# Attention probabilities turned by VectorE and DMA instead of by TensorE

## The chip, the cores and the metric

One Trainium2 chip, one core of it. The metric is the device time of one execution in microseconds (us). The core's engines run in parallel, each through its own queue in order: TensorE (PE in the rows, with its weight loads as PEld), VectorE (DVE), ScalarE (ACT), GpSimd (POOL) and SyncE (SP), which issues most DMAs. They wait for one another through semaphores.

## The reference

One block on x of 512 positions by 2048 channels, in fp32, depth 1:

```
h = rms_norm(x);  q, k, v, g_a, u_p, g_p = split(h @ w_in)           # six widths of 1024
q, k = rms_norm per 64 channels, then a partial rotation by position
s_c = q_c k_c^T / 8;  p_c = softmax(s_c)          # 8 heads, two halves c = 0, 1 of 64 channels
a = p_0 - lam * p_1;  o = a @ v;  attn = rms_norm(o) * 0.8
pool = (centred_mean(u_p, window) - u_p) @ w_pool * pool_scale        # windows 2, 4, 8, 16
out = x + concat(attn * silu(g_a), pool * silu(g_p)) @ w_out
```

## The kernel before

**Precision.** Every fp32 operand of a product is split in two: ScalarE writes a rounded high part (fp32r), VectorE the rest as a low part, and TensorE does three products (high x high, low x high, high x low) instead of one. So each tile of weights costs ScalarE one cast of 128 x 512 and VectorE one subtraction.

**Halves.** Weights come in blocks of 512 KB (`raw`, four slots) and are split in halves of 128 x 512 into four slots (`w_hi`, `w_lo`). One half feeds twelve products of 128 x 512 on TensorE. ScalarE's split of half m + 3 waits until TensorE has ended half m - 1 (semaphore `w_used`), since it takes that half's slot.

**Stages.** First V for all heads (32 halves), then K of the first round (8), then four rounds over m = 8 ... 47. A round has five groups of 8 halves: Q, U (the pool's input), GA, GP (the gates), and K of the next round, each into two PSUM banks. In the last round the output product begins in place of K; then follow six more passes of it.

**A round's attention.** Two heads of four query tiles make eight items. They are woven between the halves by hand: each engine has a loop over m with tests on m. Before the change, item i goes like this:
- TensorE, after half 24 + 2i: the scores of the 128 queries against 512 keys, 4 products into banks S0 and S0 + 1 (`scored`). They wait for the exponentials of item i - 1 (`exp_done`), which read the same banks.
- VectorE, m = 25 + 2i: the row maximum (L1063) and its scaling (L1064).
- ScalarE, m = 26 + 2i: behind the split of half m + 3 (L685) the cast at_hi of item i - 1 (L799), and then two exponentials with row sums (L806, item i).
- VectorE, m = 27 + 2i: reciprocal, coefficient, scaling by a vector (L1044), and p_0 - lam p_1 (L1046).
- TensorE, after half 27 + 2i: four transposes of 128 x 128 into bank TB (L584).
- VectorE, m = 28 + 2i: at_lo (L1070).

After half 35 and after half 43 TensorE multiplies the four turned items of a head with V (12 products). After half 39 it does the pool's 12 products, and at m = 40 it waits for VectorE's evacuation of GP's bank (L926) before K's first half. The sums for K and Q are normalised and rotated by VectorE up to m = 22 (L958 to L965), and SyncE copies parts of Q and K to the other 64 partitions (L347 to L357).

**Start.** TensorE runs 16 products on ones (L452). SyncE issues x in parts of 512 KB and 1 MB (L286), V's weights (L293), and then twelve DMAs of constants (L329, L331) before it goes on with V's weights. The row of epsilons is spread by one fp32 product (L625) and copied by VectorE.

All products but these go through one helper (L457).

Of the kernel before, what the change touches and what calls it, by code (L numbers as in the profile page):

```python
# [6 lines left out]
F32 = mybir.dt.float32  # L7
# [16 lines left out]
def hybrid_block(nc, x, x_cols, norm_w, w_in, q_norm_w, k_norm_w, lq1, lk1, lq2, lk2, subln_w, w_pool,  # L24
                 pool_scale, w_out, identity, pair_ones, rope_cos, rope_sin, inv_count, out):
# [34 lines left out]
    with ExitStack() as ctx:  # L60
# [28 lines left out]
        q_stack, q_stack_at = fixed("q_stack", [P, 2, 2, SEQ], F32R)  # L89
        kh_twice, _ = fixed("kh_twice", [P, 2, 2, SEQ], F32R)  # L90
        kl_twice, _ = fixed("kl_twice", [P, 2, 2, SEQ], F32R)
        diff, diff_at = fixed("diff", [P, 2, 2, SEQ], F32R)
        at_hi, at_hi_at = fixed("at_hi", [P, ST, SEQ], F32R)
        at_lo, _ = fixed("at_lo", [P, ST, SEQ], F32R)
        work, work_at = fixed("work", [P, 5 * 2 * XW])
        wp_raw, wp_raw_at = fixed("wp_raw", [P, 512])
        inv_cnt, inv_cnt_at = fixed("inv_cnt", [P, SEQ])
# [3 lines left out]
        wp_hi, _ = fixed("wp_hi", [P, 512], F32R, at=inv_cnt_at)  # L101
# [3 lines left out]
        wide_b, _ = fixed("wide_b", [P, KP - RAW_SLOTS, HN], at=at_hi_at)  # L105
# [8 lines left out]
        hsq_hi, hsq_lo = kh_twice[:, 0, 1], kl_twice[:, 0, 1]  # L114
# [7 lines left out]
        x_eps = sb("x_eps", [P, ST])  # L122
        nw = sb("nw", [P, KT])
        cos_t = sb("cos_t", [P, SEQ])
        sin_t = sb("sin_t", [P, SEQ])
        ident = sb("ident", [P, P])
# [16 lines left out]
        row_max = sb("row_max", [P, 2])  # L143
# [3 lines left out]
        coef = sb("coef", [P, 1])  # L147

# [42 lines left out]
        eps_diag, ones_f32 = probs[:, 0, :], gate[:, 0, 0:P]  # L191
        rstd_line = head_out[0:1, :]
# [14 lines left out]
        x_in = [sem(f"x_in{i}") for i in range(5)]  # L207
        x_row_in = [sem(f"x_row_in{i}") for i in range(ST)]
        rstd_squared = sem("rstd_squared")
        eps_diag_ready, eps_spread, eps_row_ready = sem("eps_diag_ready"), sem("eps_spread"), sem("eps_row_ready")  # L210
        x_rstd_ready, rstd_line_in, rstd_spread = sem("x_rstd_ready"), sem("rstd_line_in"), sem("rstd_spread")
        sums_raised, gate_ready, pool_gate_ready = sem("sums_raised"), sem("gate_ready"), sem("pool_gate_ready")
        ident_in, k_moved = sem("ident_in"), sem("k_moved")
# [7 lines left out]
        wp_in, inv_in, scale_in = sem("wp_in"), sem("inv_in"), sem("scale_in")  # L221
# [6 lines left out]
        scored, max_ready, exp_done, attn_ready = sem("scored"), sem("max_ready"), sem("exp_done"), sem("attn_ready")  # L228
        at_transposed, at_hi_ready, at_lo_ready = sem("at_transposed"), sem("at_hi_ready"), sem("at_lo_ready")
# [32 lines left out]
        def form_count(p, pair):  # L262
            return (KP // 2) * p + pair + 1

# [19 lines left out]
        def _(sp):  # L284
# [30 lines left out]

            load_x_cols(0, 0, 2)
            load_v(0)
            load_x_cols(1, 2, 4)
            load_v(1)
            load_x_cols(2, 4, 8)  # L320
            load_v(2)
# [993 lines left out]
```

## Time and profile before

| | us |
|---|---|
| median of 3 runs | 777.97 (777.52 to 778.23) |
| the profiled execution, its own time | 778.13 |
| its span in the profile | 776.3 |
| TensorE busy | 769.8 |
| VectorE busy | 551.0 |
| ScalarE busy | 381.6 |
| GpSimd busy | 31.3 |

The span runs from the first to the last instruction; the profiled execution takes 1.8 us more than its span. Busy times overlap. The granted clock is full in every slice of the page. A product of 128 x 512 shows as some 390 ns, but products overlap and follow one another every 0.23 us.

### The profile page before, as it was taken

The numbers are of one execution on the slowest core, as the hardware profiler recorded it, in microseconds if no ns is written. First come the engines' busy times: TensorE is split into PE (matmuls) and PEld (weight loads), VectorE is DVE, ScalarE is ACT, GpSimd is POOL, SyncE is SP. The second block draws the span as 40 slices with busy tenths as digits, with TensorE's granted clock in tenths as the row PEclk, the third lists the DMA queues.
The fourth block names the chain that finished last, engine by engine and source line by source line (L and its number), as shares of the span: only waits on it lengthen the run. The fifth ranks groups of instructions, "written<-read, shape, count | busy, mean of one in ns | idle before, by whom it ended". The sixth has DMA issues, their size and how long they took to land.

```text
span 776.3 us, 9638 instructions
## 1 busy us (share of the span) xinstructions
PE 769.8 (99%) x3458; PEld 637.0 (82%) x3458; DVE 551.0 (71%) x861; ACT 381.6 (49%) x649; POOL 31.3 (4%) x42
## 2 busy tenths in 40 slices
PE   9999999999999999999999999999999999999997
PEld 8788888888888888888888888888888888888886
DVE  5543235888854788985478897348888869987796
ACT  5463134444474354455354355554345665655552
POOL 0010000000000000000000000000000003322200
PEclk9999999999999999999999999999999999999999
DMA  9853323452222354221234421224432169999972
GB/s 333 327 194 92 98 89 102 135 156 70 74 73 64 109 149 126 78 81 55 81 110 147 122 81 57 79 78 139 140 105 81 56 233 255 276 275 263 211 168 108
DMA packets 67079, 106.22 MB, mean 137 GB/s; under 512 B 5344, under 2 KB 46560, under 8 KB 66528
## 3 DMA queue, kind: packets, MB, share of 16 engines
q1 hardware_dynamic: 60288, 86.72, 34.6%
q0 software_dynamic: 4736, 16.78, 11.0%
q10 hardware_dynamic: 2016, 2.18, 0.9%
q8 instruction: 27, 0.44, 0.2%
q14 instruction: 12, 0.10, 0.0%
HBM read 95.17 MB, written 4.19 MB: 128 GB/s over the span
## 4 chain that ended last, share of the span: by engine, by line
PE 96%; SPq 2%; DMA 1%; issue 0%; DVE 0%; ACT 0%
PE ps L457 94%; PE ps L584 2%; DMA raw<-in_w_in 1%; SPq L329 1%; SPq L286 1%; SPq L293 0%; SPq L331 0%; PE ps L625 0%; DVE x_left L1213 0%; ACT w_hi L675 0%
## 5 line engine op out<-in xcount | busy, mean ns | idle before, releaser
L903 DVE TENSOR_TENSOR w_lo<-raw,w_hi 128x512 fp32r<-128x512 f32 x240 | 163.4, 689 | 166.3 <-ACT w_hi L685 90.8
L457 PE MATMUL ps<-h_hi,w_hi 128*128 128x512 f32 x640 | 251.0, 392 | 0.0
L457 PE MATMUL ps<-h_lo,w_hi 128*128 128x512 f32 x640 | 249.3, 390 | 0.0
L457 PE MATMUL ps<-h_hi,w_lo 128*128 128x512 f32 x640 | 171.2, 389 | 0.0
L685 ACT CAST w_hi<-raw 128x512 fp32r<-128x512 f32 x149 | 90.6, 621 | 156.2 <-PE ps L457 155.4
L457 PEld LDWEIGHTS ps<-h_hi,w_lo 128*128 128x128 f32 x640 | 120.1, 188 | 25.1
L457 PEld LDWEIGHTS ps<-h_hi,w_hi 128*128 128x128 f32 x640 | 120.2, 188 | 24.6
L457 PEld LDWEIGHTS ps<-h_lo,w_hi 128*128 128x128 f32 x640 | 120.2, 188 | 24.5
L457 PE MATMUL ps<-w_hi,h_hi 128*128 128x512 f32 x352 | 122.0, 391 | 1.5 <-ACT w_hi L675 1.5
L457 PE MATMUL ps<-w_hi,h_lo 128*128 128x512 f32 x352 | 121.4, 389 | 0.0
L457 PE MATMUL ps<-w_lo,h_hi 128*128 128x512 f32 x352 | 121.4, 389 | 0.0
L457 PEld LDWEIGHTS ps<-w_hi,h_hi 128*128 128x128 f32 x352 | 65.9, 188 | 16.3 <-issue 2.6
L457 PEld LDWEIGHTS ps<-w_hi,h_lo 128*128 128x128 f32 x352 | 66.1, 188 | 13.8
L457 PEld LDWEIGHTS ps<-w_lo,h_hi 128*128 128x128 f32 x352 | 66.1, 188 | 13.6
L675 ACT CAST w_hi<-raw 128x512 fp32r<-128x512 f32 x43 | 26.3, 620 | 61.1 <-PE ps L457 50.2
L806 ACT ACTIVATE probs<-ps,neg_max 128x512 f32<-128x512 f32 x64 | 43.6, 690 | 0.0
L744 ACT CAST w_hi<-raw 128x512 fp32r<-128x512 f32 x48 | 29.1, 622 | 24.2 <-PE ps L457 21.3
L1063 DVE TENSOR_REDUCE row_max<-ps 128x2 f32<-128x1024 f32 x32 | 39.0, 1218 | 0.0
L435 POOL DMA_DIRECT2D raw<-in_w_out x12 | 10.4, 870 | 606.0 <-DVE w_lo L903 602.9
L744 ACT CAST w_hi<-tall 128x512 fp32r<-128x512 f32 x32 | 19.9, 623 | 19.4 <-PE ps L457 19.4
L1070 DVE TENSOR_TENSOR at_lo<-ps,at_hi 128x512 fp32r<-128x512 f32 x32 | 21.9, 685 | 8.7 <-ACT at_hi L799 8.7
L744 ACT CAST w_hi<-wide_b 128x512 fp32r<-128x512 f32 x32 | 19.8, 623 | 16.7 <-PE ps L457 16.7
(143 smaller groups left out, 785.4 us busy)
## 6 DMA issues: line engine op xcount, KB each, us to landing
raw<-in_w_in SPq DMA_DIRECT2D x96, 512.0 KB, 3.7
raw<-in_w_out SPq DMA_DIRECT2D x12, 512.0 KB, 3.8
raw<-in_w_out POOLq DMA_DIRECT2D x12, 512.0 KB, 17.0
wide_b<-in_w_out POOLq DMA_DIRECT2D x12, 512.0 KB, 18.7
x_rows<-in_x SPq DMA_DIRECT2D x4, 1024.0 KB, 12.8
tall<-in_w_out SPq DMA_DIRECT2D x8, 512.0 KB, 13.1
tall<-in_w_out POOLq DMA_DIRECT2D x8, 512.0 KB, 23.4
mixed<-in_x_cols SPq DMA_DIRECT2D x3, 1024.0 KB, 13.2
```

What stands on the lines that cost most here:

```text
L286: sp.dma_start(x_turned[:, a:b, :], x_col_tiles[:, a:b, :]).then_inc(x_in[n], 16)
L329: sp.dma_start(dst, src).then_inc(const_in, 16)
L435: pool.dma_start(w_tile(p, j), w_block(row, col, j), accum_op=ALU.add).then_inc(wide_added[j], 16)
L457: last = nc.tensor.matmul(dst, lhs, rhs, start=first and i == 0, stop=final and i == len(pairs) - 1, skip_group_check=True)
L584: last = nc.tensor.transpose(ps[:, TB, t * P:(t + 1) * P], probs[:, 0, t * P:(t + 1) * P], ident[:, :])
L675: nc.scalar.copy(w_hi[:, n % W_SLOTS, :], raw[:, unit % RAW_SLOTS, part * 512:part * 512 + 512]).then_inc(w_hi_ready, 1)
L685: nc.scalar.copy(w_hi[:, m % W_SLOTS, :], raw[:, unit % RAW_SLOTS, part * 512:part * 512 + 512]).then_inc(w_hi_ready, 1)
L744: nc.scalar.copy(w_hi[:, h % W_SLOTS, :], src).then_inc(w_hi_ready, 1)
L806: nc.scalar.activation(probs[:, c, :], ps[:, S0 + c, :], ACT.Exp, bias=neg_max[:, c:c + 1], scale=SCALE, accum_out=row_sum[:, c:c + 1]).th ...
L903: nc.vector.tensor_tensor(w_lo[:, slot, :], src, w_hi[:, slot, :].bitcast(F32), ALU.subtract).then_inc(w_lo_ready, 1)
L1063: chain(nc.vector.reduce_max(row_max[:, :], ps[:, S0:S0 + 2, :], AX_X))
L1070: nc.vector.tensor_tensor(at_lo[:, :, t * P:(t + 1) * P], ps[:, TB, :].rearrange("p (t s) -> p t s", t=ST), at_hi[:, :, t * P:(t + 1) * P] ...
```

## The change

- The transposes on TensorE are gone. VectorE turns an item's 128 x 512 in blocks of 32 x 32 (`transpose`), into `turned`; then four DMAs of 64 KB put the blocks on the right partitions, two from SyncE (in its queue before the weight load of the unit) and two from GpSimd (whose queue holds nothing else then).
- For this the keys stand in another order: K is written by residue modulo 4 (`p h (c j)` from `p h (j c)`), and K's copies get another layout. The product with V reads at_hi and at_lo in runs of 32 columns (`key_tile`).
- The scaling by 1/sum goes from VectorE to ScalarE, after p_0 - lam p_1. ScalarE at m = 24 + 2i now does: split, scaling of item i - 1, cast at_hi of item i - 2, exponentials of item i. VectorE waits for the scaling before it turns the item.
- Items start two halves earlier (scores after half 22 + 2i, maximum at 23 + 2i, before the split); the maximum's scaling is folded into Q's weights and `negate`.
- Head 1 gets its own slots of at_hi and at_lo in part (item_place), with waits; hsq_hi, hsq_lo, wide_b lie elsewhere, and wide_b's loads come after the unit loop.
- The pool's window sums are done only as far as a round needs them, with ratios on the 8 edge columns instead of a row of counts.
- VectorE's loop over rounds is written out.
- Start: x and the first weights in parts of 256 KB, the first half of the weights on ScalarE's queue, constants later, 9 warming products instead of 16; GpSimd spreads the epsilons, L625 and its copy are gone.

The core of the diff:

```diff
+        def item_place(i):
+            return (i, i) if i < ST else ((i + 2 - ST) % ST, (i + 2 - ST) % ST + 2)
...
+            def move_item(rnd, i):
+                slot = item_place(i)[1]
+                sp.wait_ge(at_turned, rnd * ITEMS + i + 1)
+                for a in range(ST // 2):
+                    sp.dma_start(at_raw[:, slot, a * P:(a + 1) * P],
+                                 turned[32 * a:32 * a + 32, slot, :]).then_inc(at_moved[i % 2], 16)
...
+                    if unit >= 10 and unit - 10 < ITEMS:
+                        move_item(r, unit - 10)
...
+            for r in range(ROUNDS):
+                for i in range(ITEMS):
+                    slot = item_place(i)[1]
+                    pool.wait_ge(at_turned, r * ITEMS + i + 1)
+                    for a in range(ST // 2, ST):
+                        pool.dma_start(at_raw[:, slot, a * P:(a + 1) * P],
+                                       turned[32 * a:32 * a + 32, slot, :]).then_inc(at_moved_2[i % 2], 16)
...
+            def key_tile(split, h, t):
+                slots = split[:, 2 * h:2 * h + ST, :]
+                return slots.rearrange("p s (a t i) -> p t s a i", a=ST, t=ST)[:, t].rearrange("p s a i -> p (s a) i")
...
-                        for t in range(ST):
-                            last = nc.tensor.transpose(ps[:, TB, t * P:(t + 1) * P],
-                                                       probs[:, 0, t * P:(t + 1) * P], ident[:, :])
-                        last.then_inc(at_transposed, 1)
...
-                    nc.tensor.matmul(ps[:, 0, :], ones_f32, eps_diag, start=True, stop=True).then_inc(eps_spread, 1)
...
+                    i, odd = divmod(m - 24, 2)
+                    if 1 <= i <= ITEMS and not odd:
+
+                        slot = item_place(i - 1)[1]
+                        act.wait_ge(at_mixed, r * ITEMS + i)
+                        nc.scalar.activation(at_raw[:, slot, :], at_raw[:, slot, :], ACT.Copy, scale=row_inv[:, 0:1]
+                                             ).then_inc(at_scaled, 1)
+                    if 2 <= i < ITEMS + 2 and not odd:
+
+                        slot = item_place(i - 2)[1]
+                        for moved in (at_moved[i % 2], at_moved_2[i % 2]):
+                            act.wait_ge(moved, r * (ITEMS // 2 * ST * 8) + ((i - 2) // 2 + 1) * ST * 8)
+                        nc.scalar.copy(at_hi[:, slot, :], at_raw[:, slot, :]).then_inc(at_hi_ready, 1)
...
-                        nc.vector.tensor_tensor(wk(0), wk(2), wk(1), ALU.add).then_inc(qk_rotated, 1)
+                        nc.vector.tensor_tensor(wk(0).rearrange("p h (c j) -> p h j c", c=4),
+                                                wk(2).rearrange("p h (j c) -> p h j c", c=4),
+                                                wk(1).rearrange("p h (j c) -> p h j c", c=4), ALU.add
+                                                ).then_inc(qk_rotated, 1)
...
-                        chain(nc.vector.tensor_scalar(probs[:, 0, :], probs[:, 0, :], row_inv[:, 0:1], None,
-                                                      ALU.mult))
...
+                    if 0 <= i < ITEMS and not odd:
+                        dve.wait_ge(scored, r * ITEMS + i + 1)
+                        nc.vector.reduce_max(neg_max[:, :], ps[:, S0:S0 + 2, :], AX_X, negate=True
+                                             ).then_inc(max_ready, 1)
...
+                    if 1 <= i <= ITEMS and not odd:
+                        dve.wait_ge(at_scaled, r * ITEMS + i)
+                        slot = item_place(i - 1)[1]
+                        nc.vector.transpose(turned[:, slot, :], at_raw[:, slot, :]).then_inc(at_turned, 1)
```

## Rows read from the trace of the kernel before

**Rows 1.** The page, part 1: busy time, share of the span, instructions.

```profile
PE 769.8 (99%) x3458; PEld 637.0 (82%) x3458; DVE 551.0 (71%) x861; ACT 381.6 (49%) x649; POOL 31.3 (4%) x42
```

**Rows 2.** Chain that ended last, in order of time: start us, us, what.

```profile
76.97 0.86 PE ps L625 x2
...
176.76 0.43 PE ps L584 x4
177.20 6.38 PE ps L457 x28
```

**Rows 3.** Timeline, one item: start us, us, engine, line, operation, out<-in, count, [idle before].

```profile
176.60 0.60 PE L584 MATMUL ps<-ident,probs 128*128 128x128 f32 x4
176.80 0.62 ACT L685 CAST w_hi<-raw 128x512 fp32r<-128x512 f32 x1 [3.01 <-PE ps L457]
...
177.32 0.58 ACT L799 CAST at_hi<-ps 128x512 fp32r<-128x512 f32 x1
...
177.80 0.70 ACT L806 ACTIVATE probs<-ps,neg_max 128x512 f32<-128x512 f32 x1
...
179.04 0.21 ACT L806 ACTIVATION_READ_ACCUMULATOR probs<-ps,neg_max 128x1 f32 x1
...
179.78 0.39 PE L457 MATMUL ps<-kh_twice,q_stack 128*128 128x512 f32 x1
```

**Rows 4.** Timeline, the start.

```profile
4.36 1.33 ACT L652 ACTIVATE h_hi<-mixed,nw 128x512 fp32r<-128x512 f32 x2 [1.34 <-DMA mixed<-in_x_cols]
...
6.55 1.14 ACT L675 CAST w_hi<-raw 128x512 fp32r<-128x512 f32 x2 [0.85 <-DMA raw<-in_w_in]
...
7.31 1.16 PE L457 MATMUL ps<-w_hi,h_hi 128*128 128x512 f32 x4 [0.44 <-ACT w_hi L675]
...
14.66 1.33 ACT L652 ACTIVATE h_hi<-mixed,nw 128x512 fp32r<-128x512 f32 x2
...
15.90 0.61 ACT L675 CAST w_hi<-raw 128x512 fp32r<-128x512 f32 x1
...
28.27 1.07 PE L457 MATMUL ps<-w_lo,h_hi 128*128 128x512 f32 x4
29.68 1.14 ACT L675 CAST w_hi<-raw 128x512 fp32r<-128x512 f32 x2 [9.32 <-DMA raw<-in_w_in]
...
30.44 1.17 PE L457 MATMUL ps<-w_hi,h_hi 128*128 128x512 f32 x4 [1.10 <-ACT w_hi L675]
```

**Rows 5.** Timeline, before the first item of round 0.

```profile
157.40 0.46 SPq L357 DMA_DIRECT2D q_stack<-q_low  x1
...
161.13 0.39 PE L457 MATMUL ps<-h_hi,w_hi 128*128 128x512 f32 x1
...
165.60 1.29 DVE L903 TENSOR_TENSOR w_lo<-raw,w_hi 128x512 fp32r<-128x512 f32 x2
...
167.53 0.39 PE L457 MATMUL ps<-h_hi,w_hi 128*128 128x512 f32 x1
```

**Rows 6.** Timeline, VectorE at m = 40 of round 0.

```profile
220.40 1.23 DVE L926 TENSOR_TENSOR work<-ps,rstd_row 128x1024 f32<-128x1024 f32 x1 [0.84 <-PE ps L457]
```

**Rows 7.** Groups of VectorE's instructions: line, operation, shapes, count, busy us, mean ns, idle before.

```profile
L1063 DVE TENSOR_REDUCE row_max<-ps 128x2 f32<-128x1024 f32 x32 | 39.0, 1218 | 0.0
...
L1044 DVE TENSOR_SCALAR probs<-probs,row_inv 128x512 f32<-128x512 f32 x32 | 15.4, 480 | 0.0
...
L963 DVE STREAM_SHUFFLE work<-work 128x512 f32<-128x512 f32 x8 | 5.8, 729 | 0.0
```

**Rows 8.** DMA issues: queue, count, KB each, median us to landing.

```profile
raw<-in_w_out POOLq DMA_DIRECT2D x12, 512.0 KB, 17.0
...
q_stack<-q_low SPq DMA_DIRECT2D x16, 128.0 KB, 3.3
...
head_out<-x_rstd POOLq DMA_DIRECT2D x4, 0.5 KB, 2.0
```

**Rows 9.** The page, part 5: GpSimd's issues, columns as rows 7.

```profile
L435 POOL DMA_DIRECT2D raw<-in_w_out x12 | 10.4, 870 | 606.0 <-DVE w_lo L903 602.9
```

More of the change, by code:

```diff
@@ L122, in hybrid_block @@
         x_eps = sb("x_eps", [P, ST])
+        x_half = sb("x_half", [P, ST])
         nw = sb("nw", [P, KT])
@@ L425, in _ @@
             nc.gpsimd.memset(ones_f32, 1.0).then_inc(ones_set, 1)
+            pool.wait_ge(x_eps_ready, 1)
+            for t in range(ST):
+                pool.dma_start(eps_line[:, t * P:(t + 1) * P], x_eps[:, t:t + 1]).then_inc(eps_line_in, 16)
             pool.wait_ge(x_rstd_ready, 1)
@@ L594, in pe_round @@
                             lo = v_all[:, (KP + 2 * r + h) * SEQ + t * P:(KP + 2 * r + h) * SEQ + (t + 1) * P]
-                            last = products(ps[:, OB, :], [(hi, at_hi[:, t, :]), (hi, at_lo[:, t, :]),
-                                                           (lo, at_hi[:, t, :])], t == 0, t == ST - 1)
+                            last = products(ps[:, OB, :].rearrange("p (s n) -> p s n", s=ST),
+                                            [(hi, key_tile(at_hi, h, t)), (hi, key_tile(at_lo, h, t)),
+                                             (lo, key_tile(at_hi, h, t))], t == 0, t == ST - 1)
                         last.then_inc(head_done, 1)
@@ L768, in act_round @@
                             rows = slice(64 * c, 64 * c + 64)
-                            nc.scalar.copy(kh_twice[rows, c], wk(0)[rows]).then_inc(qk_hi_ready, 1)
+                            nc.scalar.copy(kh_twice[rows, :, c], wk(0)[rows]).then_inc(qk_hi_ready, 1)
                     if m in (19, 21):
@@ L809, in act_round @@
+                    if 0 <= i < ITEMS and not odd:
+                        act.wait_ge(max_ready, r * ITEMS + i + 1)
+                        for c in range(2):
+                            nc.scalar.activation(probs[:, c, :], ps[:, S0 + c, :], ACT.Exp,
+                                                 bias=neg_max[:, c:c + 1], scale=1.0,
+                                                 accum_out=row_sum[:, c:c + 1]).then_inc(exp_done, 1)
                     if m == 35:
@@ L846, in _ @@
             act.wait_ge(nw_in, 16)
-            for q in range(2):
-                x_high(q)
-                split_first(2 * q)
-                split_first(2 * q + 1)
+            for kk in range(2):
+                x_high(0, (kk,))
+                split_first(kk)
+            x_high(1)
+            split_first(2)
+            split_first(3)
             for n in range(1, HALVES):
@@ L880, in _ @@
         def _(dve):
-            steps = [0]
+            steps, chained = [0], [0]
             def setup(ins):
@@ L891, in _, with x_low @@
                 dve.sem_inc(started, START)
-            def x_low(q):
-                for kk in range(2):
+            def x_low(q, parts=(0, 1)):
+                for kk in parts:
                     k = 2 * q + kk
@@ L1121, in dve_round @@
                         split_form_low(2 * m - 77)
-                assert step[0] == STEPS, step[0]
             dve.wait_ge(nw_in, 16)
-            for q in range(2):
-                x_low(q)
-                for n in (2 * q, 2 * q + 1):
-                    split_rest(n, raw_half(n), n + 1)
+            for kk in range(2):
+                x_low(0, (kk,))
+                split_rest(kk, raw_half(kk), kk + 1)
+            x_low(1)
+            for n in (2, 3):
+                split_rest(n, raw_half(n), n + 1)
             for n in range(1, HALVES):
@@ L1172, in _ @@
                     v_low(n - 2 * KT - 1, 1)
-            with dve.Fori(0, ROUNDS - 1) as r:
+            for r in range(ROUNDS - 1):
                 dve_round(r)
```

248 lines of the change are left out of this document (115 added, 133 removed).

## The prediction

> **What bounds the kernel now.** I read the page's busy shares first: TensorE is busy 99% of a 776.3 us span [rows 1]. The chain that ended last, in order of time, says the same: nearly every piece is TensorE, and the transposes stand in it as pieces of 0.43 to 0.44 us between pieces of products [rows 2]. A stretch of 28 products takes 6.38 us, 0.228 each, so a "half" (twelve products, one step of the loop over m) takes 2.73 us. Work taken from TensorE comes off the end one for one, as long as nothing makes it wait. So the second question is how late its suppliers may be. I take that from the timeline of one item [rows 3], of the first item of a round [rows 5] and of the bank handed over at m = 40 [rows 6].
>
> Below, E is the moment TensorE ends the half that releases ScalarE's next split of weights. In [rows 3] E is 176.60. ScalarE starts at E + 0.20, goes to the cast of at_hi 0.52 later, to the exponentials 0.48 later, and ends the second one's sum at 179.25, which is E + 2.65. TensorE needs it for the next scores at 179.78, after four transposes (0.44) and a half (2.73). The spare is 0.52 us. The same rows stand in the items of the other rounds.
>
> **What the change takes off TensorE.** Four transposes an item, eight items a round and four rounds make 32 sets, each 0.43 or 0.44 us in the chain [rows 2], 0.437 in the mean: 14.0 us. The product of L625 is 0.86 us [rows 2]; its row now comes from GpSimd, asked for at VectorE's step 15 and needed at step 27, twelve halves (33 us) later, which cover it. If GpSimd's broadcast took more than that, VectorE's splits would be late next.
>
> At the start, the first products run at 7.31 [rows 4], behind the first 512 KB of x (landed at 4.36) and 512 KB of weights (second landing, casts from 6.55 on, 0.76 before 7.31). Both first pieces are now half as large and come over two queues. The weights' 512 KB came 6.55 - 4.36 = 2.19 us behind those of x; with 2 x 256 KB fewer ahead, the pair should be there up to 2.19 us sooner, less what the two queues take from each other. I take 1.75 us, between ends of 1.0 (fewer warming products leave a gap) and 2.2. The stall before 30.44 is 30.44 minus 28.27 minus four products (0.91), 1.26, plus 0.10 because the first four products after it take 1.17 instead of 1.07 [rows 4]. The weights for it were issued behind twelve constants; these now go behind two more loads, so the 1.36 us should go. Left as it is, the stall would leave out 1.36 of the gain.
>
> Together: 14.0 + 0.86 + 1.75 + 1.36 = 17.97 us.
>
> At one place the Trainium skill ("VectorE: DVE Perf Modes", The three transpose paths, and its rules for kernel authors) advises TensorE for 128 x 128 and gives 390 ns for one of bf16. The chain shows 0.437 us for four of fp32, 0.109 each. By the page's price the removed work would be 49.9 us and the forecast far faster; I keep to the row.
>
> **What it puts before TensorE: ScalarE's chain.** At step m = 24 + 2i ScalarE now does the split, the scaling of item i-1, the cast at_hi of item i-2 and then the exponentials of item i. The scores of item i+1 still wait for these. The split cannot start before E. A scaled copy from SBUF has a pace of 0.62 (two of L652 from 14.66, the next cast at 15.90) [rows 4]; a cast from SBUF 0.52, as the split [rows 3]. So the exponentials end at E + 0.20 + 0.52 + 0.62 + 0.52 + 1.45 = E + 3.31. A waiting TensorE starts 0.14 after ScalarE's end (29.68 plus 0.62 against 30.44) and loses 0.10 of its overlap [rows 4]: E + 3.55. It wants to go on at E + 2.73, since the transposes no longer fill 0.44. That is a wait of 0.82 us. It holds for i = 2, 3, 4, 5, four a round. At i = 6 the head's twelve value products stand between and cover it. For i = 1 the cast is not there: E + 3.03, a wait of 0.30. The wait does not pay itself back, since ScalarE's start hangs on TensorE's last half through the four weight slots. The bounds for one event are 0.55 (scaling at 0.48, only 0.10 to restart) and 0.95.
>
> **VectorE, first item.** The scores of item 0 move from after half 24 to after half 22, at 161.13 in [rows 5]. The last move of Q is issued at 157.40 and lands 3.3 us later, at 160.7 [rows 5, 8], just in time. But VectorE is full from the rotation of Q; it comes to item 0's maximum only after the first of the two splits from 165.60, at 166.20. Then 1.22 for the maximum [rows 7], 0.03 across, 1.45 for the exponentials: 168.90, and with the restart 169.14. TensorE wants the scores of item 1 at 167.53 (scores of item 0 and halves 23 and 24 done). That is 1.61 us a round, with ends of 1.2 and 2.0. Behind VectorE's maximum stand only its own splits, which have two halves to spare. The reordered sum for K (L1025) now writes with a stride, which no row shows: at 0 extra (I take this; shape and elements are as before) it changes nothing; at twice its 1.22 us, as [rows 7] show for 1024 elements, it adds up to 1.2 to this wait, 4.9 in all.
>
> **VectorE, m = 40.** At m = 39 VectorE waits for ScalarE's scaling of item 7, which stands behind the split at E. The scaled data are there at E + 0.20 + 0.52 + 0.71 + 0.03 = E + 1.46. The transpose has no row; STREAM_SHUFFLE of the same shape takes 0.73 [rows 7], its pace about 0.65; the ends are 0.48 (the fast TENSOR_SCALAR) and 1.22. Behind it in the queue is the evacuation of GP's bank, 1.22, which now starts at E + 2.11 where it started at 220.40, the E + 0.20 of that step [rows 6]. TensorE needs that bank at step 40 and has only the pool's twelve products to do before: 2.11 + 1.22 + 0.24 - 2.73 = 0.84 us a round. Behind the same wait stand, in other steps, the next split, at_lo, a pool sum and the next maximum. There it hides: VectorE's 1.5 us of standing still per item replaces the 0.48 of the removed TENSOR_SCALAR, and it is back in time for the next maximum.
>
> **The moves.** They must land between the transpose (about E + 2.1) and the cast two steps on, 5.9 us later at the tightest. SyncE's two: 3.3 us for one of 128 KB within SBUF [rows 8], plus one more issue, under 4.5. They stand ahead of the next weight load in SP's queue, but VectorE gives that load's signal later anyway. GpSimd's two: 0.87 an issue [rows 9], then between 2.0 (small) and 17.0 (512 KB each, with the DMA engines full) [rows 8]. At 64 KB each I take 2.5, 4.3 in all: hidden. The fewer pool sums, the rounds written out on VectorE (29% of its span is idle [rows 1]) and the edge ratios cost nothing: TensorE's work covers them. The w_out blocks loaded later (wide_b) are the same bytes in the same queue in another order; if one came late, the splits of pass 1 would wait for it. The value products read their moving operand in runs of 32; no row shows such a read, so 0, with 96 times 0.228 = 21.9 us as the far end.
>
> **The sum.** Waits a round: 1.61 + 0.30 + 4 x 0.82 + 0.84 = 6.03; four rounds 24.1. Less 17.97: +6.15 us. On the profiled execution's 778.13 this is 784.3; the median of the runs, 777.97, lies 0.16 below, which I leave.
>
> **The rivals.**
> 1. Nothing waits: ScalarE's chain ends before E + 2.49 and VectorE is early. Then 778.13 - 17.97 = 760.2. For it: the spare of 0.52 today and ScalarE at half load [rows 1]. Against: the chain is serial and would have to lose 0.8 us. Chance 0.12.
> 2. The other side of no change: VectorE's two late points cost nothing (a shorter transpose and an earlier maximum), and only ScalarE's chain waits: 24.1 - 4 x (1.61 + 0.84) = 14.3, so 774.5. It decides once VectorE reaches item 0's maximum before 164.6 or so; the rows say 166.2. Chance 0.13.
> 3. GpSimd's moves are late. If each of its two issues first stands behind a VectorE instruction of 1.22 us [rows 7], they land 2 x 1.22 + 1.75 + 2.5 = 6.7 us after the transpose. That is 0.8 past the tightest window and 0.3 past the three others of a round that the chain leaves open (6.4): 4 x 0.8 + 12 x 0.3 = 6.8, so 791. It decides from 5.9 us on. Chance 0.10. The Trainium skill ("SBUF — State Buffer", two separate sides) says that VectorE's two-port instructions lock GpSimd out while it writes descriptors. The 480 ns TENSOR_SCALAR, of the fast kind, is removed by this change, and no run here shows a GpSimd issue beside it.
> 4. Strided accesses cost: 789 (K's sum) to 806 (value products). Chance 0.08.
> My forecast has 0.57; its own range is 776 to 793.
>
> **How the numbers follow.** About 0.2% (1.6 us) is what a measurement of this kernel tells from no change. Of my forecast's 0.57, 0.09 lies within that band and 0.02 below it, since the break-even point, 18.0 us of waits, is three quarters of the 24.1. Faster: 0.12 + 0.13 + 0.02 = 0.27. Same: 0.09. Slower: 0.64. The range 772 to 800 leaves out rival 1 and the far part of 3 and 4, 0.18.
>
> **What would show it.** TensorE loses the L584 and L625 rows, and its first product is near 5.6. Its idle time appears, released by ScalarE's exponentials (L806's successor): about 28 waits, 0.8 us for most, four of 1.6. Four more of 0.8 are released by VectorE's evacuation at m = 40. TensorE's share falls to about 96%. I am wrong if ScalarE's idle time ends on DMA before at_hi (rival 3), if the value products have longer rows (rival 4), or if the exponentials end before TensorE is ready (rivals 1 and 2).

## The result, and the profile after

The changed kernel takes 786.56 us (median of 4 executions, 786.45 to 788.45), the kernel before beside it 778.1 (777.52 to 780.32). The ratio is 1.0114, with a 95% interval of 1.0093 to 1.0134: 7 to 10 us slower. One execution in this document, of max_early, fell into a slow state (1059.96 us at a granted clock of 0.67); without it the median of max_early is 780.47 and not 780.75. Forecast: 784.3 in a range of 772 to 800, "slower" at 0.64. The direction and the mechanism hold. Most terms of the sum were of another size, and their errors cancel in part, so that the total came within 2.3 us is partly luck (the table below).

The profiled execution of the changed kernel took 788.45 us with a span of 786.6. It is the highest of the four, and its start is the likely reason (below). Busy time on its page, to be laid beside [rows 1]:

```profile
PE 765.2 (97%) x3314; PEld 621.5 (79%) x3314; DVE 545.3 (69%) x823; ACT 400.5 (51%) x681; POOL 68.5 (9%) x111
```

TensorE does less (769.8 before) in a longer span. 128 transposes are gone, and its idle time within the span is now 21.4 us where it was 6.5. The view of waits, for TensorE (engine and tile waited at, what for, us in all, times, longest), says what took their place:

```profile
PE ps L494 <- ACT probs L837: 11.8, 19, 1.5
PE ps L494 <- DMA q_stack<-q_low: 2.0, 3, 1.5
PE ps L494 <- DVE work L959: 1.6, 4, 0.4
PE ps L494 <- ACT w_hi L706: 1.1, 1, 1.1
```

Three of these four are new. I measure a loss as the distance between the starts of two products, less 0.227 us for each product started in between; that is some 0.26 us more for each restart than the idle time in this view.

**One item**, the one of [rows 3] (now E = 178.38), from the timeline of the changed kernel:

```profile
178.58 0.62 ACT L716 CAST w_hi<-raw 128x512 fp32r<-128x512 f32 x1 [3.27 <-PE ps L494]
...
179.11 0.72 ACT L825 ACTIVATE at_raw<-at_raw,row_inv 128x512 f32<-128x512 f32 x1
...
179.74 0.60 ACT L832 CAST at_hi<-at_raw 128x512 fp32r<-128x512 f32 x1
...
181.49 0.20 ACT L837 ACTIVATION_READ_ACCUMULATOR probs<-ps,neg_max 128x1 f32 x1
...
181.73 0.50 PE L494 MATMUL ps<-kh_twice,q_stack 128*128 128x512 f32 x1 [0.47 <-ACT probs L837]
182.07 0.40 PE L494 MATMUL ps<-kl_twice,q_stack 128*128 128x512 f32 x1
```

ScalarE's four pieces stand one behind the other as in the forecast, and the last ends at 181.69, E + 3.31 to the hundredth. TensorE loses 0.63 before the scores and 0.11 after the first of them (the next starts 0.34 behind it instead of 0.23): 0.74 where I said 0.82.

**The first item of round 0**, to be laid beside [rows 5]:

```profile
160.21 0.50 PE L494 MATMUL ps<-kh_twice,q_stack 128*128 128x512 f32 x1 [0.36 <-DMA q_stack<-q_low]
...
165.26 1.22 DVE L1086 TENSOR_REDUCE neg_max<-ps 128x2 f32<-128x1024 f32 x1
...
168.01 0.50 PE L494 MATMUL ps<-kh_twice,q_stack 128*128 128x512 f32 x1 [1.14 <-ACT probs L837]
```

The maximum starts 3.9 us after the scores of item 0 could first be read, because VectorE is busy with its splits and the rotation of Q, and the scores of item 1 wait for it: 1.4 to 1.7 us in three rounds and 0.3 in the last. The first scores wait too, for the move of Q: 0.3 to 0.6 us in three rounds and 1.8 in the last.

**VectorE at m = 40** (beside [rows 6]) and, from the page, the new groups and DMA issues (last columns: busy, mean ns, idle before; for the issues KB and us to landing):

```profile
223.07 0.71 DVE L1103 STREAM_TRANSPOSE turned<-at_raw 128x512 f32<-128x512 f32 x1 [1.78 <-ACT at_raw L825]
223.71 1.19 DVE L959 TENSOR_TENSOR work<-ps,rstd_row 128x1024 f32<-128x1024 f32 x1
```

```profile
L466 POOL DMA_DIRECT2D at_raw<-turned x64 | 34.7, 548 | 534.0 <-DVE turned L1103 533.7
...
L1103 DVE STREAM_TRANSPOSE turned<-at_raw 128x512 f32<-128x512 f32 x32 | 22.8, 711 | 45.2 <-ACT at_raw L825 45.1
...
at_raw<-turned SPq DMA_DIRECT2D x64, 64.0 KB, 2.5
at_raw<-turned POOLq DMA_DIRECT2D x64, 64.0 KB, 2.2
```

VectorE stands still 1.78 us for ScalarE's scaling and evacuates the bank only after its transpose, as forecast (0.66 lost in place of 0.84). The moves land 2.0 to 4.2 us after their issue, in a window of 5.9; at_hi never waits for one.

**The sum for K.** It has the shape and the elements of before but writes with a stride. First the row of the kernel before (all four rounds, columns as [rows 7]), then that of the changed kernel in one round; the other three take the same 2.07 us:

```profile
L1025 DVE TENSOR_TENSOR work<-work 128x1024 f32<-128x1024 f32 x4 | 4.9, 1219 | 0.0
...
140.59 2.07 DVE L1056 TENSOR_TENSOR work<-work 128x1024 f32<-128x1024 f32 x1
```

**The start**, beside [rows 4]:

```profile
0.98 4.21 PE L489 MATMUL ps<-gate 128*128 128x128 f32 x18 [0.98 <-POOL gate L449]
...
5.50 0.62 ACT L706 CAST w_hi<-raw 128x512 fp32r<-128x512 f32 x1 [0.81 <-DMA raw<-in_w_in]
...
6.26 2.05 PE L494 MATMUL ps<-w_hi,h_hi 128*128 128x512 f32 x4 [1.07 <-ACT w_hi L706]
...
8.10 1.91 PE L494 MATMUL ps<-w_hi,h_lo 128*128 128x512 f32 x4
9.81 1.26 PE L494 MATMUL ps<-w_lo,h_hi 128*128 128x512 f32 x4
10.91 1.08 PE L494 MATMUL ps<-w_hi,h_hi 128*128 128x512 f32 x4
...
29.98 1.07 PE L494 MATMUL ps<-w_hi,h_hi 128*128 128x512 f32 x4
```

The second half of the weights in the kernel before:

```profile
10.13 1.07 PE L457 MATMUL ps<-w_hi,h_hi 128*128 128x512 f32 x4
```

The first product is 1.05 us earlier than before, but the first eight take about twice their usual time (0.56 us from the first start to the second, 0.43 for each of the next seven), so the second half starts at 10.91 where it started at 10.13. The stall before 30.44 is gone: the half that started there now starts at 29.98, and its products no longer run 0.10 longer. In this execution the start gives 0.6 us in all, not 3.11.

### The profile page after: what moved, and what is told of

It is laid out like the page before. It is cut to its first block, busy times and chain, and to the rows that moved or that the text cites. A ratio compares the mean times of both kernels' runs of the same rounds, so it can differ in the third digit from the quotient of the medians.

```text
span 786.6 us, 9148 instructions
## 1 busy us (share of the span) xinstructions
PE 765.2 (97%) x3314; PEld 621.5 (79%) x3314; DVE 545.3 (69%) x823; ACT 400.5 (51%) x681; POOL 68.5 (9%) x111
## 4 chain that ended last, share of the span: by engine, by line
PE 69%; DVE 14%; ACT 10%; issue 4%; DMA 2%; ACTq 1%; DVEq 0%
PE ps L494 69%; ACT probs L837 3%; ACT at_raw L825 2%; DVE w_lo L936 2%; DVE work L1018 1%; ACT work L730 1%; ACT work L728 1%; DMA q_stack<-q_low 1%; ACT at_hi L832 1%; DVE q_low L984 1%; DVE work L1056 1%; ACT w_hi L716 1%; DVE work L1052 1%; DVE work L1046 1%; DVE work L1041 1%
## 5 line engine op out<-in xcount | busy, mean ns | idle before, releaser
L466 POOL DMA_DIRECT2D at_raw<-turned x64 | 34.7, 548 | 534.0 <-DVE turned L1103 533.7
L1103 DVE STREAM_TRANSPOSE turned<-at_raw 128x512 f32<-128x512 f32 x32 | 22.8, 711 | 45.2 <-ACT at_raw L825 45.1
L494 PE MATMUL ps<-kh_twice,q_stack 128*128 128x512 f32 x64 | 28.1, 438 | 13.9 <-ACT probs L837 11.8
L1086 DVE TENSOR_REDUCE neg_max<-ps 128x2 f32<-128x1024 f32 x32 | 39.0, 1219 | 1.7 <-PE ps L494 1.4
L494 PEld LDWEIGHTS ps<-kh_twice,q_stack 128*128 128x128 f32 x64 | 12.0, 187 | 26.9 <-ACT probs L837 17.8
## 6 DMA issues: line engine op xcount, KB each, us to landing
tall<-in_w_out SPq DMA_DIRECT2D x8, 512.0 KB, 13.1
```

What stands on the lines that cost most here:

```text
L466: pool.dma_start(at_raw[:, slot, a * P:(a + 1) * P], turned[32 * a:32 * a + 32, slot, :]).then_inc(at_moved_2[i % 2], 16)
L494: last = nc.tensor.matmul(dst, lhs, rhs, start=first and i == 0, stop=final and i == len(pairs) - 1, skip_group_check=True)
L1086: nc.vector.reduce_max(neg_max[:, :], ps[:, S0:S0 + 2, :], AX_X, negate=True).then_inc(max_ready, 1)
L1103: nc.vector.transpose(turned[:, slot, :], at_raw[:, slot, :]).then_inc(at_turned, 1)
```

## The experiments

Times are medians; "before" is the kernel before, run in the same session. The changed kernel itself was not run again, so the last column compares sessions; between them the kernel before moved by up to 0.5 us, and the two intervals of turn7_late and the changed kernel overlap. For differences of 2 us or less the traces decide. Each change is one to the changed kernel unless said.

| kernel | us | before | ratio to before (95%) | against 786.56 |
|---|---|---|---|---|
| scale_vec | 773.53 | 778.34 | 0.9931 (0.9909 to 0.9953) | -13.0 |
| exp_first | 778.43 | 778.34 | 0.9998 (0.9979 to 1.0017) | -8.1 |
| max_early | 780.75 | 778.34 | 1.0021 (0.9999 to 1.0044) | -5.8 |
| warm16 | 786.65 | 778.34 | 1.0098 (1.0068 to 1.0127) | +0.1 |
| turn7_late | 784.44 | 778.19 | 1.0078 (1.0054 to 1.0102) | -2.1 |
| order_plain | 783.52 | 778.19 | 1.0065 (1.0042 to 1.0088) | -3.0 |
| all_fixes | 765.37 | 778.19 | 0.9825 (0.9797 to 0.9854) | -21.2 |
| before_1turn | 769.93 | 778.19 | 0.9887 (0.9858 to 0.9916) | (-8.3 to before) |
| no_moves | 788.22 | 778.59 | 1.0114 (1.0083 to 1.0144) | +1.7 |
| pool_moves | 788.40 | 778.59 | 1.0127 (1.0099 to 1.0154) | +1.8 |
| fixes_warm9 | 766.26 | 778.59 | 0.9847 (0.9818 to 0.9876) | -20.3 |

### The scaling back on VectorE: scale_vec

```diff
-                        nc.scalar.activation(at_raw[:, slot, :], at_raw[:, slot, :], ACT.Copy, scale=row_inv[:, 0:1]
-                                             ).then_inc(at_scaled, 1)
...
+                        nc.vector.tensor_tensor(coef[:, :], row_inv[:, 1:2], neg_lam[:, :], ALU.mult)
+                        chain(nc.vector.tensor_scalar(probs[:, 0, :], probs[:, 0, :], row_inv[:, 0:1], None,
+                                                      ALU.mult))
...
-                        dve.wait_ge(at_scaled, r * ITEMS + i)
+                        dve.wait_ge(at_mixed, r * ITEMS + i)
```

> The changed kernel with the scaling by 1/sum taken back to VectorE (a TENSOR_SCALAR of 128x512 on the first exponentials, as in the kernel before); ScalarE keeps the split, the cast of at_hi and the exponentials. My theory (the waits before the scores come from the length of ScalarE's serial chain, in which the scaling has 0.62 us): the exponentials end at E + 2.69 in place of E + 3.31, so each of the sixteen waits of 0.73 us shrinks to about 0.11, the wait at i = 1 (0.21) goes, and the wait at m = 40 (0.66) goes, since VectorE's transpose of item 7 no longer stands behind ScalarE: 16 x 0.62 + 4 x 0.21 + 4 x 0.66 = 13.4 us less than the changed kernel, about 773. The rival (VectorE is the late one and the scaling only fills time in which ScalarE would wait for the maximum anyway): no gain, 786, or more, as VectorE has 0.48 us more an item.

Measured: 773.53. The timeline of the same item has ScalarE's chain without its second piece, and TensorE's wait is gone; only the slower restart (0.34 between the first two products) is left:

```profile
178.51 0.62 ACT L716 CAST w_hi<-raw 128x512 fp32r<-128x512 f32 x1 [3.00 <-PE ps L494]
179.03 0.61 ACT L830 CAST at_hi<-at_raw 128x512 fp32r<-128x512 f32 x1
...
180.80 0.20 ACT L835 ACTIVATION_READ_ACCUMULATOR probs<-ps,neg_max 128x1 f32 x1
...
181.05 0.50 PE L494 MATMUL ps<-kh_twice,q_stack 128*128 128x512 f32 x1
181.39 0.40 PE L494 MATMUL ps<-kl_twice,q_stack 128*128 128x512 f32 x1
```

So 32 scalings of 0.62 us on an engine that is busy half the time cost the kernel 13 us, because of where they stand. This edit alone makes the kernel faster than before.

### The same work in another order: exp_first

```diff
-                    if 2 <= i < ITEMS + 2 and not odd:
...
-                        nc.scalar.copy(at_hi[:, slot, :], at_raw[:, slot, :]).then_inc(at_hi_ready, 1)
                     if 0 <= i < ITEMS and not odd:
...
                                                  accum_out=row_sum[:, c:c + 1]).then_inc(exp_done, 1)
+                    if 2 <= i < ITEMS + 2 and not odd:
...
+                        nc.scalar.copy(at_hi[:, slot, :], at_raw[:, slot, :]).then_inc(at_hi_ready, 1)
```

> The changed kernel with the order of two pieces on ScalarE exchanged in each step: split, scaling of item i-1, exponentials of item i, and only then the cast at_hi of item i-2. Nothing is taken away. My theory (order and length of ScalarE's chain ahead of the exponentials set the wait): the exponentials end 0.52 us earlier, E + 2.79; sixteen waits of 0.73 us shrink to about 0.21, so 8.3 us less than the changed kernel, about 778; the waits at m = 40 and before the second scores of a round stay. The rival (ScalarE's total work an item, 3.1 us in a window of 6.4 us, or the late at_hi and at_lo then hold VectorE's next maximum back): no gain.

Measured: 778.43, with no instruction removed. In the view of waits the 19 for the exponentials are down to the four before the second scores of a round:

```profile
PE ps L494 <- ACT probs L831: 4.9, 4, 1.6
PE ps L494 <- DVE work L959: 1.6, 4, 0.4
```

The sixteen waits at i = 2 to 5 were made by position, not by load: no work was taken from ScalarE. What is left of each is a slower restart of 0.2 to 0.3 us. The rival, that a later at_hi and at_lo hold VectorE back, is out.

### The first maximum of a round earlier: max_early

```diff
+                    if m == 21:
+                        dve.wait_ge(scored, r * ITEMS + 1)
+                        nc.vector.reduce_max(neg_max[:, :], ps[:, S0:S0 + 2, :], AX_X, negate=True
+                                             ).then_inc(max_ready, 1)
...
-                    if 0 <= i < ITEMS and not odd:
+                    if 1 <= i < ITEMS and not odd:
                         dve.wait_ge(scored, r * ITEMS + i + 1)
```

> The changed kernel with the maximum of each round's item 0 moved on VectorE from step 23 to step 21, ahead of a split that finds VectorE idle for 1.37 us in the trace of the changed kernel. My theory (the wait before the second scores of a round comes from VectorE's late maximum): the maximum ends near 162.6 in place of 166.5 in that round, the exponentials follow the next split of ScalarE, and the 1.40, 1.59, 1.73 and 0.28 us that TensorE lost there go: about 4.5 to 5 us less than the changed kernel, about 782. The wait for Q's move before item 0 (0.3 to 1.8) stays. The rival (ScalarE would be late there anyway, as in the other items): under 2 us.

Measured: 780.75, a gain of 5.8 us where about 5 were expected. The maximum now stands where VectorE was idle, and the scores of item 1 start with no wait:

```profile
160.96 1.23 DVE L1070 TENSOR_REDUCE neg_max<-ps 128x2 f32<-128x1024 f32 x1
162.20 0.69 DVE L936 TENSOR_TENSOR w_lo<-raw,w_hi 128x512 fp32r<-128x512 f32 x1
...
166.23 0.39 PE L494 MATMUL ps<-kh_twice,q_stack 128*128 128x512 f32 x1
```

### The evacuation ahead of the last transpose: turn7_late

```diff
                         scale_evac(wk(0), GP).then_inc(evacuated, 1)
+                        dve.wait_ge(at_scaled, r * ITEMS + ITEMS)
+                        slot = item_place(ITEMS - 1)[1]
+                        nc.vector.transpose(turned[:, slot, :], at_raw[:, slot, :]).then_inc(at_turned, 1)
...
-                    if 1 <= i <= ITEMS and not odd:
+                    if 1 <= i < ITEMS and not odd:
```

> The changed kernel with VectorE's wait and transpose of item 7 moved from step 39 to step 40, behind the evacuation of the bank that TensorE asks for. Nothing is taken away. My theory (the 0.66 us before half 40 comes from that wait and transpose standing ahead of the evacuation): the four waits go, 2.6 us less than the changed kernel, 783.9. The rival (the evacuation is late for another reason, as the split of step 39): nothing gained.

Measured: 784.44, 2.1 us less. In its trace the evacuation comes first, and half 40 starts without a wait:

```profile
219.90 1.23 DVE L959 TENSOR_TENSOR work<-ps,rstd_row 128x1024 f32<-128x1024 f32 x1 [0.51 <-PE ps L494]
221.17 0.71 DVE L1032 STREAM_TRANSPOSE turned<-at_raw 128x512 f32<-128x512 f32 x1
```

### Keys in plain order: order_plain

```diff
-                slots = split[:, 2 * h:2 * h + ST, :]
-                return slots.rearrange("p s (a t i) -> p t s a i", a=ST, t=ST)[:, t].rearrange("p s a i -> p (s a) i")
+                return split[:, 2 * h + t, :]
...
-                        nc.vector.tensor_tensor(wk(0).rearrange("p h (c j) -> p h j c", c=4),
-                                                wk(2).rearrange("p h (j c) -> p h j c", c=4),
-                                                wk(1).rearrange("p h (j c) -> p h j c", c=4), ALU.add
+                        nc.vector.tensor_tensor(wk(0), wk(2), wk(1), ALU.add
```

> The changed kernel without the ordering of the keys by residue: the sum of K's rotation writes plainly, and the value products read a contiguous 128x512 operand. The order of the keys within the value products is therefore not the reference's; the work is the same. My theory (the strided write takes 2.07 us in place of 1.22, and pushes VectorE's work up to item 0's maximum back by 0.85 us): the waits for Q's move before item 0 go (2.0 to 3 us in all), those before item 1 shrink by 0.8 us a round, and the value products go back from 0.2375 to 0.2268-0.23 us each (0.9 us in all): 6 us less than the changed kernel, 780.5. The rival (VectorE has slack there, 0 as I took it in the prediction): only the 0.9 us.

Measured: 783.52, 3.0 us less, half of what I expected. The sum is back at 1.22 us, and so is the pace of the value products:

```profile
L1055 DVE TENSOR_TENSOR work<-work 128x1024 f32<-128x1024 f32 x4 | 4.9, 1218 | 0.0
...
L494 PE MATMUL ps<-at_hi,v_all 128*128 128x512 f32 x64 | 21.0, 389 | 0.0
```

But VectorE gives half of the 0.85 us back: its next two splits now wait 0.58 and 0.83 us for ScalarE, where it waited 1.19 once. It comes out 0.44 us earlier, so the waits for Q's move go in three rounds (in the fourth 1.4 us stay) and the one before item 1 stays at 1.5 to 1.6. My theory of the stride holds, its price was too high: by the losses in the two traces 1.7 us for the waits, and 1.0 for the products.

### The start: warm16 and fixes_warm9

```diff
-WARM = 9
+WARM = 16
```

> The changed kernel with 16 warming products in place of 9, as the kernel before has. In the changed kernel the first half's products run at 0.43 to 0.46 us each after a gap of 1.07 us behind the last warming product, and the second half starts at 10.91 us. My theory (TensorE is granted its slow pace for longer after the shorter warming and the gap): the first half takes about 2.7 us from 6.3 on, the second starts near 9.0, and the kernel is about 1.9 us faster, 784.7. The rival (the pace at the start is set by how the data of x and of the weights arrive): the second half starts at 10.9 again and nothing is gained.

Measured: 786.65; by its time nothing gained. Its trace shows the forecast pace all the same:

```profile
6.56 1.18 PE L494 MATMUL ps<-w_hi,h_hi 128*128 128x512 f32 x4
...
9.41 1.07 PE L494 MATMUL ps<-w_hi,h_hi 128*128 128x512 f32 x4
```

The traces of the other kernels say more. With 9 warming products the slow pace is there in four profiled executions (the changed kernel, scale_vec, max_early, no_moves: second half at 10.5 to 11.1 us) and absent in five (exp_first, turn7_late, order_plain, pool_moves, fixes_warm9: 8.8 to 9.1). In the first group, those of the changed kernel, scale_vec and no_moves were the slowest executions of their kernel; in the second, exp_first, pool_moves and fixes_warm9 the fastest. The two groups differ before the first half begins. Here is the row of the warming products from fixes_warm9, to be laid beside that of the changed kernel above:

```profile
0.98 3.95 PE L489 MATMUL ps<-gate 128*128 128x128 f32 x18 [0.98 <-POOL gate L449]
```

They take 4.21 us in all four traces of the first group, and none of their 18 pieces takes under 421 ns. In the five of the second they take 3.70 to 4.16, and the shortest piece takes 274 to 374 ns. So in the second group TensorE had gone over to its faster pace before the warming products ended, in the first it had not, and the first half begins at the pace at which the warming ended. The gap does not sort them: 0.96 to 1.29 us in the first group, 1.07 to 1.57 in the second.

With 16 the slow pace is absent in all four traces (warm16, all_fixes, the kernel before, before_1turn), and in each the shortest warming piece takes 274 or 275 ns; but the products start later. That would explain the times: three executions of the changed kernel at 786.45 to 786.64 with the fast start and one at 788.45 with the slow one, so that 16 warming products can't improve on the median and take away only the slower execution (six executions of warm16 lie between 786.2 and 787.2). Only the profiled executions have traces; for the others this is inferred from their times. To see two groups I ran the four edits with 9.

> The kernel with the four edits together (765.4) but with the changed kernel's 9 warming products in place of 16. The traces so far show the first half's products at 0.43 us in three kernels with 9 (second half at 10.5 to 11.1 us) and at 0.227 us in three others with 9 (second half at 8.8 to 9.1), never at 0.43 with 16 (9.4 to 10.3). My theory (after 9 warming products and a gap the pace of the first half differs from one execution to the next): the executions fall in two groups about 1.9 us apart, the faster one about 0.5 us below the four-edit kernel's 764.4, the slower near 766. The rival (the pace belongs to the kernel, not to the execution): one group.

Measured: 765.58, 765.94, 766.57 and 767.79. The one with the fast start is the lowest, but four executions don't fall into two groups, and the spread for other reasons is as large. That the pace belongs to the execution and not to the kernel rests on the nine traces, whose kernels share the start and differ behind it, and not on this run.

### The moves: no_moves and pool_moves

no_moves leaves out the DMAs of the blocks, so these stay on the partitions on which they were turned; pool_moves gives all four of an item to GpSimd.

```diff
 no_moves
-                        for moved in (at_moved[i % 2], at_moved_2[i % 2]):
-                            act.wait_ge(moved, r * (ITEMS // 2 * ST * 8) + ((i - 2) // 2 + 1) * ST * 8)
+                        act.wait_ge(at_turned, r * ITEMS + i - 1)
 pool_moves
-                    for a in range(ST // 2, ST):
+                    for a in range(ST):
```

> The changed kernel without the moves of blocks between partitions (no DMA from SyncE or GpSimd for the probabilities; the cast at_hi waits for VectorE's transpose alone), so the blocks stay on the partitions on which they were turned. My theory (the moves land 2.2 to 4.2 us after their issue, in a window of 5.9 to 6.4 us, and are hidden; they slow nothing else): the time stays within 1 us of the changed kernel, 786.5. Rival 3 of the prediction (GpSimd's moves are late) or contention of their 4 x 64 KB an item with the loads of weights: 3 to 7 us less.

> The changed kernel with all four moves of an item issued by GpSimd, in place of two by GpSimd and two by SyncE. By my theory the last lands 4 x 0.548 + 2.2 = 4.4 us after the transpose, or 6.2 with the longest landing in the trace (4.2 us), against a window of 5.9 to 6.4: within 1 us of 786.5. Rival 3 (GpSimd's issues are held up by VectorE's instructions, by 1.22 us each): 4 x 1.22 longer, 8.4 us after the transpose, at least 2 us late in each of sixteen items, 820.

Measured: 788.22 and 788.40, outside the 1 us I had allowed around 786.5, though the ratios are as that of the changed kernel (1.0114 and 1.0127 against 1.0114). For no_moves the start is the likely reason: three of its four executions lie at 788.1 to 788.4, one at 786.1, and the profiled one, at 788.43 with the slow start, stands beside 788.45 of the changed kernel with the same start. Without any move nothing is gained. For pool_moves, the profiled execution with the fast start took 787.12, some 0.6 us more than the three of the changed kernel at 786.45 to 786.64. From its trace, four issues in 2.2 us:

```profile
178.92 2.20 POOL L462 DMA_DIRECT2D at_raw<-turned  x4 [4.40 <-DVE turned L1098]
```

```profile
at_raw<-turned POOLq DMA_DIRECT2D x128, 64.0 KB, 3.2
```

Its median landing is 3.2 us behind the issue, the longest 4.5. And here the moves are at the edge of their window: the last cast at_hi of each round waits 0.4 to 0.7 us for one. TensorE does not wait for these four casts, but three of its waits before scores are 0.1 to 0.2 us longer than the others of their kind. In the changed kernel no cast waits for a move, so rival 3 is out for it; with all four moves on GpSimd the margin is gone.

### The transposes alone: before_1turn

```diff
-                        for t in range(ST):
+                        for t in range(1 if i else ST):
                             last = nc.tensor.transpose(
```

> The kernel before with one of the four transposes of an item instead of four (items 1 to 7 of each round; item 0 keeps all four), so three quarters of the transposed blocks are stale; nothing else changes. It measures what transposes taken from TensorE are worth by themselves. If each is worth its 0.109 us: 28 x 3 x 0.109 = 9.2 us less than the kernel before, 769.1. If ScalarE's chain, whose spare of 0.52 us contained 0.44 us of transposes, then makes TensorE wait, the gain is smaller: the spare left is 0.52 - 0.33 = 0.19 us, so I expect no such wait. If a transpose costs more than its row shows (a longer one is suggested by the price in the Trainium skill): 30 us less.

Measured: 769.93, 8.3 us less than before for 84 transposes taken out (in the profiled executions 8.1; of the remaining 1, 0.2 is a later start, and no new wait shows). In the timelines an item's two steps go from 6.82 to 6.49 us, 0.11 a transpose; the times give 0.10.

### Four edits together: all_fixes

> The changed kernel with four edits together: scaling on VectorE, exponentials ahead of the cast at_hi, the maximum of item 0 at step 21, 16 warming products. If the waits are separate, as my theory has them, the measured gains of the single edits add up: 13.0 for the scaling, 5.8 for the early maximum, 1.5 at the start (from the traces), and 1.7 more for the order (sixteen remainders of 0.11 us), 22.0 us less than 786.5: 764.5. What is left of TensorE's idle time is the wait for Q's move before item 0 (0.2 to 1.8 us a round). The rival (a supplier behind the ones removed becomes late: VectorE, with 0.48 us more an item, or at_lo before the value products): 768 or more.

Measured: 765.37 against a forecast of 764.5. The gains add up. The page and the waits of TensorE:

```profile
PE 757.7 (99%) x3328; PEld 624.0 (82%) x3328; DVE 555.3 (73%) x855; ACT 383.7 (50%) x649; POOL 68.9 (9%) x111
```

```profile
PE ps L494 <- DMA q_stack<-q_low: 1.1, 3, 0.4
PE ps L489 <- POOL gate L449: 1.0, 1, 1.0
PE ps L494 <- ACT probs L829: 0.7, 1, 0.7
```

TensorE is back at 99%, and the kernel is 1.5 to 2.0% faster than before: the transposes on VectorE pay once the work around them is ordered for TensorE's next request. Not all of it is theirs. In the profiled executions TensorE is 2.6 us ahead of the kernel before after its first 400 products, which is the start and L625, and 11.7 us at the last product; the other 9.2 are what is left of the transposes' 14.0. What remains are the losses before the first scores of a round, which wait for Q's move (0.4 to 0.7 us), and one wait of 0.7 us for the exponentials in the last round.

## Why the prediction was right, and where it was not

Terms of the sum in us, as forecast, and as read from the profiled execution or shown by the run named:

| term | forecast | measured | from |
|---|---|---|---|
| 32 sets of transposes | -14.0 | -14.0 (-12.6 by the times) | before_1turn, 0.10 to 0.11 each |
| product of L625 | -0.86 | -0.86 | its row is gone, nothing waits there |
| start and stall | -3.11 | -0.6; -2.4 to -2.8 at the fast pace | start rows; the five traces with the fast pace |
| before items 0 and 1 | +6.4 | +8.2 | losses; max_early took 5.8 away |
| i = 1 | +1.2 | +0.9 | losses |
| i = 2 to 5 | +13.1 | +12.0 | losses; scale_vec, exp_first |
| m = 40 | +3.4 | +2.6 | losses; turn7_late took 2.1 away |
| longer steps of products | 0 | +1.8 | 2.5 in place of 0.7 us above 0.227 a step, summed |
| sum | +6.15 | +10.0 (profiled execution: +10.3) | |

With the fast start, which by their times three of the four executions had, the sum is about +8, and the medians differ by 8.5, with an interval of 7.2 to 10.4. Against that the forecast missed by 2.3 us. Single terms missed by as much as 1.8 in both directions: the start, items 0 and 1 and the longer products made the kernel slower than I said, ScalarE's chain and m = 40 made it less slow. That these partly cancel is luck.

- **ScalarE's chain.** Right, and shown twice: by taking a piece out (scale_vec) and by the order alone (exp_first). The chain's length was exact. The wait was 0.08 too large, for the most part because TensorE starts 0.04 us behind ScalarE's end (181.73 against 181.69) and loses 0.11 after it, 0.15 in all, where I took 0.24 from the one stall of the start [rows 4].
- **VectorE at item 0.** Right in its place (max_early) and near in its size: 1.4 to 1.7 us in three rounds against 1.61. I missed that the move of Q, which I called just in time, is late in every round (0.3 to 0.6 us, and 1.8 in the last). In part that is the strided sum of K: order_plain takes the late move away in three rounds. This step of the prediction ("at 0 extra (I take this)") failed: the sum takes 0.85 us more; it named the far end (twice 1.22), and 2.07 lies near that.
- **m = 40.** Right. With the restart at 0.15 in place of 0.24 the estimate of 0.84 would have been 0.75, against 0.66 measured. The transpose has a pace of 0.64 us (223.07 to 223.71), as taken from STREAM_SHUFFLE.
- **The start.** The step that failed most in the profiled execution. The pieces came sooner, 1.05 us for the first product, but I had treated the products behind it as having their usual pace, and counted fewer warming products as nothing but a gap. In this execution the first eight products ran at half the pace: 8 x 0.21 = 1.7 us lost. In five other traces of kernels with 9 they did not, and there TensorE had reached the faster pace before the warming ended. Why it does so sooner in one execution than in another is open.
- **Strided reads.** I put the reads in runs of 32 at 0. They cost 0.010 us a product, 1.0 us in all, against a far end of 21.9: the 12 products of a head now take 2.84 us from start to start (0.2368 each), and 2.72 (0.2267 each) in order_plain. Another 0.8 us is spread thinly over halves; its cause was not found.
- **The rivals.** Rival 1 (nothing waits, 760.2) and rival 2 (774.5) need earlier suppliers than this change has; the four edits come to 765.4 that way. Rival 3 is out by the trace of the changed kernel and by no_moves. Rival 4 had the right mechanism for both, at 1.7 us for K's sum and not 4.9, and at 1.0 for the value products and not 21.9.

Two places where the Trainium skill was weighed. "VectorE: DVE Perf Modes", The three transpose paths, gives 390 ns for a 128x128 transpose of bf16 on TensorE. An estimate by that figure, 84 x 0.39, is 33 us for before_1turn, and it gained 8.3: the trace does not agree, and the measurement decides. Inside a stream of products the row of the chain, 0.109 us each, is the price. Its preference for TensorE is borne out for the changed kernel as it stands and not for all_fixes. "SBUF — State Buffer", two separate sides, says that GpSimd is locked out, and cannot write descriptors, while VectorE runs an instruction in a two-port mode. Here its issues took 548 ns each and landed after 2.2 us in the median, 4.2 at most. But in the traces of the changed kernel, scale_vec, all_fixes and pool_moves no issue of a move ran beside one of VectorE's TENSOR_SCALARs, the kind the prediction had in mind, so no run here shows such a lock or excludes it.

## What to carry to other kernels

Work taken off the bounding engine pays only as long as its suppliers keep their lead, and the work removed was itself part of that lead: the spare before the scores was 0.52 us, 0.44 of it the transposes. Before moving work to a half-idle engine, write down that engine's serial order between the event that releases it and the piece that the bound waits for, and put the moved work behind that piece. Here one reordering of three pieces was worth 8 us, as much as the whole change had cost; the piece itself was not the trouble, its place was.

## What the runs showed of the hardware

- VectorE's sum of 128x1024 fp32 takes 2.07 us when it writes with a stride of 128 elements and 1.22 when it writes contiguously (both inputs as before). The Trainium skill ("Advanced Engine Details and Errata", Memory Cachelines) says that each access to another 16-byte line costs; the trace agrees.
- TensorE's read of a moving operand in runs of 32 fp32 costs 4% of pace: 0.2368 against 0.2267 us a product of 128x512.
- VectorE's transpose of 128x512 fp32 in 32x32 blocks takes 0.71 us, 0.64 to the next instruction.
- A DMA of 64 KB within SBUF lands 2.2 us after its issue from GpSimd and 2.5 from SyncE, and 3.2 when GpSimd issues four in a row (medians).
- After 9 warming products TensorE's first products (seven to nine of them) took 0.43 us each, the very first 0.56, in four of nine profiled executions, those in which no warming product had yet run at the faster pace. That is twice the usual 0.227, as its lower level (1.2 GHz in place of 2.4) would give, yet the profile's granted clock reads 1.00 in that stretch. With 16 warming products none of four traces had it.
